# A permuted walk through streamed columns and accumulator columns in six of eight ring slots of a hybrid decoder trunk

## The reference

```python
def swiglu_ffn(h, w_in, w_out):
    gate, up = jnp.split(h @ w_in, 2, axis=-1)
    return (jax.nn.silu(gate) * up) @ w_out

h = jnp.concatenate([meta, x], axis=1)
for i in range(DEPTH):
    h = layer_norm(DEEPNORM_ALPHA * h + 0.5 * swiglu_ffn(h, ffn_w_in[i, 0], ffn_w_out[i, 0]), ...)
    mix = short_conv_mixer(h, ...) if i % 2 == 0 else gla_mixer(h, ...)
    h = layer_norm(DEEPNORM_ALPHA * h + mix, ...)
    h = layer_norm(DEEPNORM_ALPHA * h + 0.5 * swiglu_ffn(h, ffn_w_in[i, 1], ffn_w_out[i, 1]), ...)
return h[:, N_META:]
```

## Time and profile before

| what | us |
|---|---|
| median of 2 runs | 1020.49 (1018.95 and 1022.03) |
| the profiled execution, its own time | 1018.82 |
| its span, first to last instruction | 1017.1 |
| mean granted TensorE clock, share of full | 0.998 |

### The profile page before, as it was taken

One profiled execution on the slowest core, in us unless ns is written; L12 is line 12 of the kernel. 1 busy time (PEld: TensorE's weight loads), 2 busy tenths in 40 slices (PEclk: granted clock), 3 DMA queues, 4 the chain that ended last, 5 costly groups with the idle time before them and its releaser, 6 DMA issues.

```text
span 1017.1 us, 18997 instructions
## 1 busy us (share of the span) xinstructions
PE 1004.7 (99%) x7866; PEld 983.9 (97%) x7866; DVE 723.6 (71%) x1078; ACT 512.4 (50%) x746; POOL 122.2 (12%) x136
## 2 busy tenths in 40 slices
PE   9999999999999999999999999999999999999997
PEld 7999999999999999999999999999989999999885
DVE  5865656689889865557697565667897999766444
ACT  5634344465456543444565434445867766444430
POOL 2000002320002000003220000133152420000000
PEclk9999999999999999999999999999999999999999
DMA  9965656637762966556639665555355738866531
GB/s 255 261 191 171 179 154 179 191 91 211 224 174 82 253 183 175 170 163 179 193 91 256 175 183 155 168 165 160 84 146 145 206 106 247 249 193 201 171 121 41
DMA packets 324263, 176.58 MB, mean 174 GB/s; under 512 B 6658, under 2 KB 320048, under 8 KB 324176
## 3 DMA queue, kind: packets, MB, share of 16 engines
q1 hardware_dynamic: 323664, 174.15, 59.3%
q0 software_dynamic: 480, 1.15, 0.4%
q10 hardware_dynamic: 32, 0.07, 0.0%
HBM read 174.29 MB, written 1.05 MB: 172 GB/s over the span
## 4 chain that ended last, share of the span: by engine, by line
PE 91%; DVE 4%; ACT 1%; issue 1%; POOL 1%; DMA 1%; SPq 0%; POOLq 0%; DVEq 0%; ACTq 0%
PE bank L1311 23%; PE bank L1306 23%; PE bank L1309 23%; PE bank L1325 3%; PE bank L1327 3%; PE bank L1326 3%; PE bank L1469 2%; PE bank L1471 2%; PE bank L1470 2%; PE bank L1350 2%; PE bank L1351 2%; PE bank L1352 2%; DVE weights_lo L821 1%; DMA raw_weights<-in_ffn_w_in_dram 1%; DVE rms L1219 1%
## 5 line engine op out<-in xcount | busy, mean ns | idle before, releaser
L462 ACT ACTIVATE weights_hi<-raw_weights 128x1024 fp32r<-128x1024 f32 x335 | 353.9, 1059 | 410.7 <-PE bank L1311 299.6
L821 DVE TENSOR_TENSOR weights_lo<-raw_weights,weights_hi 128x1024 fp32r<-128x1024 f32 x334 | 415.4, 1250 | 202.9 <-ACT weights_hi L462 201.7
L1306 PE MATMUL bank<-x_hi,weights_hi 128*128 128x272 f32 (+1 forms) x1584 | 226.5, 285 | 0.0
L1311 PE MATMUL bank<-x_lo,weights_hi 128*128 128x272 f32 (+1 forms) x1584 | 225.9, 285 | 0.0
L1309 PE MATMUL bank<-x_hi,weights_lo 128*128 128x272 f32 (+1 forms) x1584 | 223.9, 284 | 0.0
L1306 PEld LDWEIGHTS bank<-x_hi,weights_hi 128*128 128x128 f32 x1584 | 206.3, 188 | 0.6 <-ACT consts L628 0.2
L1311 PEld LDWEIGHTS bank<-x_lo,weights_hi 128*128 128x128 f32 x1584 | 206.9, 188 | 0.0
L1309 PEld LDWEIGHTS bank<-x_hi,weights_lo 128*128 128x128 f32 x1584 | 205.2, 188 | 0.0
L1306 PE MATMUL bank<-mid_hi,weights_hi 128*128 128x272 f32 x462 | 68.2, 288 | 0.0
L1309 PE MATMUL bank<-mid_hi,weights_lo 128*128 128x272 f32 x462 | 68.1, 288 | 0.0
L1311 PE MATMUL bank<-mid_lo,weights_hi 128*128 128x272 f32 x462 | 68.0, 288 | 0.0
(11 more groups left out here) (231 smaller groups left out, 1197.8 us busy)
## 6 DMA issues: line engine op xcount, KB each, us to landing
raw_weights<-in_ffn_w_in_dram SPq DMA_DIRECT2D x176, 512.0 KB, 4.7
raw_weights<-in_ffn_w_out_dram SPq DMA_DIRECT2D x70, 512.0 KB, 4.2
raw_weights<-in_conv_w_in_dram SPq DMA_DIRECT2D x24, 512.0 KB, 4.0
raw_weights<-in_gla_w_in_dram SPq DMA_DIRECT2D x24, 512.0 KB, 3.9
raw_weights<-in_ffn_w_out_dram SPq DMA_DIRECT2D x24, 384.0 KB, 3.5
raw_weights<-in_conv_w_out_dram SPq DMA_DIRECT2D x8, 512.0 KB, 4.9
raw_weights<-in_gla_w_out_dram SPq DMA_DIRECT2D x8, 512.0 KB, 5.0
x_tok<-in_x_dram SPq DMA_DIRECT2D x2, 512.0 KB, 5.3
```

Source lines behind the costliest of these rows:

```text
L462: nc.scalar.activation(w_hi[:, n % RING, :], raw[:, n % RAW, :], ACT.Copy).then_inc(hi_split, 1)
L821: nc.vector.tensor_tensor(w_lo[:, s, :], raw[:, n % RAW, :], w_hi[:, s, :].bitcast(F32), ALU.subtract).then_inc(lo_split, 1)
L1306: nc.tensor.matmul(ps, block_of(w_hi, n, k - k0), hi[:, k, cols], start=first and k == k0, stop=False)
L1311: mm = nc.tensor.matmul(ps, block_of(w_hi, n, k - k0), lo[:, k, cols], start=False, stop=last and k == k1 - 1)
```

## The change

For a unit in ring slot 1 to 6, `multiply` in its plain form hands the streamed operand and the PSUM range to the engine with their columns in another order, the same for both, so that each result lands where it did. A range of columns is cut in groups of `step` words and each group in runs of `run` words. The walk takes the first run of every group, then the second run of every group, and so on. With 272 columns the steps and runs in words are: slot 1: 16 and 4; slot 2: 8 and 4; slot 3: 68 and 4; slot 4: 136 and 4; slot 5: 16 and 8; slot 6: 136 and 8. With 256 columns 68 and 136 become 64 and 128. Slots 0 and 7 stay as they were. In `last_projection` the four banks get runs of 4 words with steps of 4 (which is the plain order), 16, 8 and 128 words, on the streamed weights and on PSUM. No instruction is added or taken away; the stationary operands, the other form of `multiply`, `multiply_raw` and all other engines keep theirs.

```diff
+    APART = {1: (16, 4), 2: (8, 4), 3: (T // 4, 4), 4: (T // 2, 4), 5: (16, 8), 6: (T // 2, 8)}
...
+            def spread(ap, n):
+                if n % RING not in APART:
+                    return ap
+                step, run = APART[n % RING]
+                if ap.shape[-1] != T and step > 16:
+                    step = step * SEQ // T
+                return ap.rearrange("p (i j e) -> p j i e", e=run, j=step // run)
+
             def multiply(ps, n, source, cols, k0=0, k1=KU, first=True, last=True, ready=None, before_last=None, middles=()):
 
                 hi, lo = source
                 if ready is None and before_last is None and not middles:
+                    into = spread(ps, n)
                     pe.wait_ge(hi_split, n + 1)
                     for k in range(k0, k1):
-                        nc.tensor.matmul(ps, block_of(w_hi, n, k - k0), hi[:, k, cols], start=first and k == k0, stop=False)
+                        nc.tensor.matmul(into, block_of(w_hi, n, k - k0), spread(hi[:, k, cols], n), start=first and k == k0, stop=False)
                     pe.wait_ge(lo_split, n + 1)
                     for k in range(k0, k1):
-                        nc.tensor.matmul(ps, block_of(w_lo, n, k - k0), hi[:, k, cols], start=False, stop=False)
+                        nc.tensor.matmul(into, block_of(w_lo, n, k - k0), spread(hi[:, k, cols], n), start=False, stop=False)
                     for k in range(k0, k1):
-                        mm = nc.tensor.matmul(ps, block_of(w_hi, n, k - k0), lo[:, k, cols], start=False,
+                        mm = nc.tensor.matmul(into, block_of(w_hi, n, k - k0), spread(lo[:, k, cols], n), start=False,
                                               stop=last and k == k1 - 1)
                     mm.then_inc(unit_used, 1)
                     return
...
                 def accumulate(k, b, half, first, last):
                     toks, cols = slice(META + b * P, META + (b + 1) * P), slice(half * D // 2, (half + 1) * D // 2)
-                    ps, slot = bank[4 + 2 * b + half][:], (OUT_UNIT + k) % RING
-                    nc.tensor.matmul(ps, mid_hi[:, k, toks], w_hi[:, slot, cols], start=first, stop=False)
-                    nc.tensor.matmul(ps, mid_hi[:, k, toks], w_lo[:, slot, cols], start=False, stop=False)
-                    return nc.tensor.matmul(ps, mid_lo[:, k, toks], w_hi[:, slot, cols], start=False, stop=last)
+                    slot = (OUT_UNIT + k) % RING
+                    step = (4, 16, 8, 128)[2 * b + half]
+
+                    def apart(ap):
+                        return ap.rearrange("p (i j e) -> p j i e", e=4, j=step // 4)
+
+                    ps, part_hi, part_lo = apart(bank[4 + 2 * b + half][:]), apart(w_hi[:, slot, cols]), apart(w_lo[:, slot, cols])
+                    nc.tensor.matmul(ps, mid_hi[:, k, toks], part_hi, start=first, stop=False)
+                    nc.tensor.matmul(ps, mid_hi[:, k, toks], part_lo, start=False, stop=False)
+                    return nc.tensor.matmul(ps, mid_lo[:, k, toks], part_hi, start=False, stop=last)
```

## The result

The changed kernel takes 1034.17 us (1034.12 and 1034.22) against 1020.49 us: ratio 1.0141, interval 1.0115 to 1.0167. That is slower by 1.4%, clear of the noise of these runs and inside the 2% band. The forecast was 1020 us with no change. The time lies inside its range of 985 to 1150 us, and at the upper edge of the likeliest case's own range (1008 to 1035), but a clear loss was measured where none was forecast.

A forecast was written before the change was run, and what follows sets the result against it. TensorE was taken as the bound (99% busy, 91% of the chain). The profiled 1018.8 us plus 0 for the change, plus 1.7 us to the median of the runs, gave 1020 us, range 985 to 1150.

The forecast's parts named there:

- the likeliest case: The walk's order costs nothing on the touched matmuls: 1020 us, own range 1008 to 1035, chance 0.36.
- the free order: On touched matmuls, aligned groups of 4 words are read once and addressed without regard to the last: 0 us, chance 0.36.
- sign of being wrong: Any slot's unit off by more than 0.15 us from slots 0 and 7, or those two moving themselves.
- Between them I take 0: Price of 287,880 address breaks in the touched matmuls: 0 us, between bounds of 968 and 1546 us for the kernel.
- point of decision: Price per address break in the touched matmuls, 0.07 ns (20 us over 287,880 breaks), deciding between same and slower.
- some up and some down by half, say 5 ns: Matmul time beyond a column a period (10.9 ns at 272 columns) shifts in six slots, about 10 us of mixed sign.
- B: Some steps clash, hitting one or two of the six slots: 35 us more, 1055 us, chance 0.17.
- A: Every address break in the touched matmuls loses one period, 0.417 ns: 120 us more, 1139 us, chance 0.14.
- C: Leaving a stretch of 64 words costs 2.5 ns in touched matmuls: 375 us more, 1394 us, chance 0.06.
- D: The stream of the touched matmuls falls to half rate: 1546 us, chance 0.06.
- F: The steps are merged away when the instruction is made, so nothing changes: 1020 us, chance 0.03.
- E: Short runs shrink touched matmuls' time beyond a column a period; two thirds of it gone: 985 us, chance 0.18.

The follow-up runs named there:

- run 6: Kernel before, with the last FFN's packed activations read plain from words 0, 8, 16 to 56 in ring slots 0 to 7 instead of word 48: 1022.95 us.
- run 4: Kernel before, with walks mostly in runs of 2 words (272 columns), runs of 4 to 64 (256 columns), other steps in the last projection: 1348.93 us.
- run 10: Kernel before, with runs of 2 words on the stream alone or PSUM alone, for 272 columns and the last projection: 1101.14 us.
- run 9: Kernel before, with the last FFN's first product streamed in runs of 4 words, 64 to 124 words apart by slot, PSUM plain: 1024.28 us.
- run 5: Changed kernel, with nearly all weight loads of the plain form and last projection taking 32 of the 128 columns: 1029.45 us in one run.
- run 2: Kernel before, with PSUM alone walked as in the changed kernel and the streamed operand plain: 1018.47 us in one run, beside 1018.86.
- run 8: Changed kernel, with slots 3, 4 and 6 and the last bank plain: 1020.27 us, ratio 1.002 to the kernel before.

## Why the prediction was wrong

**What held.** The bound, and nearly so that each nanosecond on a touched matmul is one on the end: TensorE's chain share went from 91% to 92%, and of its 17.0 us more 15.4 reached the end, as two waits in GLA took up the rest. The counts held (4638 and 198 matmuls). That the excess over a column a period depends on the address where a stream starts was the right trail: run 6 shows it within 64 words. It is not the whole of it, as run 4 has one start at two paces.

**The range and the sign.** That the time lies inside the range of the free order is no success of its reason: several prices and one gain came to 1.4% together. The 2% that the text took as the least that can be told from no change was too wide, as the interval is 0.26% to each side. Its own sign of being wrong did show, but only just: with 272 columns the slowest unit, 3.12 us, is 0.14 us from slots 0 and 7, inside the 0.15; the last FFN gave it, with 3.27 against 2.72 us.

**The step that failed** is "Between them I take 0" for the price of a break, with its reason "an address is made for each without regard to the last, the walk's order is free". Half of the reason fits: runs of 2 words nearly double the cost (runs 4 and 10), as if groups of 4 words were what the stream fetches. That such groups must lie at multiples of 4 words wasn't tested, as all runs of 4 or 8 words began there. But from group to group the order is not free. With runs of 4 words a jump by a multiple of 64 words costs some 0.4 to 0.5 ns, and a step of 16 words gains 1.2 to 2.6 ns a matmul against the plain order with 272 columns and 6 to 11 ns with 512, while it loses 1.2 ns against the packed 256. The net over 287,880 breaks is 15.4 us or 0.053 ns a break, under the 0.07 ns that the text gave as the point of decision; the average hides slots from -1.3 ns a matmul to +22.7.

**The second failure** is in the paragraph on the excess: "some up and some down by half, say 5 ns" and "of mixed sign". The sizes were near for 272 columns (-1.3 to +5.8 ns), but the signs don't cancel, and with 256 columns steps of 64 and 128 words were +22.7 and +13.3. A slot whose walk jumps by 64 words was priced as if it drew its excess at random, where the step decides it.

**The rivals.** B, that some steps clash, is what happened: the slots differ with their steps and not with their runs alone, in the direction it gave. Its price was 35 us against 15 measured, as no slot fell to half rate. A is out: slot 1 has 68 breaks in a matmul of 272 columns and is faster than plain. C is out by run 9: leaving a stretch of 64 words costs nothing of note, arriving at the same place in another one does. D is out for runs of 4 and 8; runs of 2 came near it. F is out, as the slots moved. E holds in one slot: step 16 takes away 1.3 of the 10.9 ns of excess in slot 1, and 11 of 20 ns in the last projection, not two thirds everywhere. Of its mechanisms the weight load beside the stream was tested in run 5 and gives 0.9 ns on average.

**The pages.** PSUM in runs of 4 and of 2 words cost nothing (runs 2 and 10). The Trainium skill, Advanced Engine Details and Errata, section "Memory Cachelines", has two sentences on that, and the measurement decides for the second, that every two consecutive elements should be adjacent, against the first, that any non-contiguous pattern slows matmuls. For SBUF it says that at least two hits on a line of 16 bytes absorb the latency. Runs 4 and 10 don't agree for a float32r stream: two adjacent words of a line and then a jump cost nearly double, 242 against 124 ns; runs of four didn't.

**What stays open.** What in SBUF repeats every 64 words, and why a stream would meet itself there, wasn't tried apart from showing that neither PSUM nor, for the most part, the weight load is the partner. The work of other engines isn't either, by the trace of the changed kernel: sixteen of the seventeen units of slot 4 with 272 columns from `x` have 130.0 ns a matmul each, while VectorE is busy for 67% to all of the unit and ScalarE for 11% to 90% of it. The price for each jump holds for runs of 4 alone: in run 4 step 64 with run 8, 24 jumps, was no slower than the plain slot. The price of step 136, which is 8 words off a multiple of 64 (+5.8 ns in slot 4), is more than J = 72 suggests in run 9 (+3.0 ns above J = 80, for 48 jumps), though its backward jumps are 132 words, 4 off a multiple. Nor is it known why start 48 is the best plain start, or what lets a plain unit of 256 columns fall into 113 or 118 ns.

## What to carry to other kernels

Read a full-rate float32r matmul by the distance of its starts and compare it with its columns at 2.4 GHz: here 6 to 10% lay between them, and they moved with the order of addresses. Keep the streamed operand in runs of at least 4 words (all runs here began at a multiple of 4 words), keep the jump between runs away from multiples of 64 words, and where the plain walk pays an excess try a step of 16 words, which costs no instruction (here 1.1% of the kernel with the packed product left plain). PSUM's side could be permuted with it for nothing here, so that the results still land in order. Try it on the whole kernel, as a unit's time also depends on the units ahead of it.

## What the runs showed of the hardware that was not expected

- A plain stream isn't the fastest order. With 512 columns from a weight slot, step 16 in runs of 4 takes 222 ns and the plain order 233 ns; the columns alone are 213 ns at 2.4 GHz.
- One start address of eight, word 48, saves 3.7 to 6.0 ns on a plain matmul of 256 columns (113.7 against 117.4 to 119.7 ns), in the order of units of run 6.
- Jumps of 64 words in runs of 4 give 134.6 ns a matmul where jumps of 68 words give 117.1, with the same number of runs and jumps.
- A plain unit's time depends on what runs ahead of it: with 272 columns up to 1.0 ns a matmul more behind a permuted unit (runs 4 and 8), with 256 packed columns 117.8 against 113.3 ns in run 4, kept through all 24 matmuls.
